# Decays without GpSimd, and key norms formed with the tokens on the partitions, in an RWKV and grid-attention block

## What is computed

```python
dx = token_shift(h) - h
x_r, x_w, x_k, x_v, x_a, x_g = (h + dx * mu[i] for i in range(6))
r = x_r @ w_in[:, c[0]:c[1]]          # k, v, g likewise from x_k, x_v, x_g
w_lo = jnp.tanh(x_w @ w_in[:, c[4]:c[5]])
a_lo = x_a @ w_in[:, c[5]:c[6]]
w_raw = (w0 + w_lo @ w_up).astype(f32)
log_decay = -jnp.exp(-jax.nn.softplus(-w_raw) - 0.5)
a = jax.nn.sigmoid((a0 + a_lo @ a_up).astype(f32))
kk = heads(k * k_k)                    # 16 heads of 64
kk = kk / jnp.maximum(jnp.sqrt(jnp.sum(kk * kk, axis=-1, keepdims=True)), 1e-12)
k = k * (1.0 + (a - 1.0) * k_a)
# recurrence over the tokens with r, decay, k, v, kk, kk * a; group norm;
# plus a bonus: sum(r * k * r_k) * v; times silu(g); @ w_out
```

## Time and profile before

| | us |
|---|---|
| median of 3 runs | 852.97 |
| lowest and highest run | 852.89, 855.48 |
| profiled execution, whole time | 856.66 |
| its span (first to last instruction) | 854.9 |
| TensorE busy in the span | 767.1 (90%) |
| VectorE, ScalarE, GpSimd busy | 501.7, 301.5, 213.0 |

### The profile page before, as it was taken

The page is one execution under the profiler, slowest core; times in us unless marked ns, Lnnn a source line. Parts: engine busy times, 40 slices in busy tenths (PEclk is TensorE's granted clock), DMA queues, the critical chain, the costliest instruction groups (busy, mean ns, idle before and its releaser), DMA issues.

```text
span 854.9 us, 17443 instructions
## 1 busy us (share of the span) xinstructions
PE 767.1 (90%) x7500; PEld 619.0 (72%) x7500; DVE 501.7 (59%) x800; ACT 301.5 (35%) x627; POOL 213.0 (25%) x163
## 2 busy tenths in 40 slices
PE   2599999799699698888876899999997999998997
PEld 2188777677578587778864788887775777776697
DVE  3983898888958622345745212631896676663611
ACT  6334542455522112233342134611333444433300
POOL 0164430444724212223211000370000000001652
PEclk9799999899889778989987999999998999999999
DMA  8023234223246764430004041601221111122131
GB/s 234 25 75 99 74 92 129 74 75 82 69 98 134 184 209 143 136 110 10 4 3 148 4 144 67 125 25 50 75 84 40 50 50 50 51 98 75 62 100 50
DMA packets 116621, 72.82 MB, mean 85 GB/s; under 512 B 26816, under 2 KB 113984, under 8 KB 116544
## 3 DMA queue, kind: packets, MB, share of 16 engines
q1 hardware_dynamic: 98496, 65.12, 26.4%
q10 hardware_dynamic: 18048, 6.58, 3.2%
HBM read 64.35 MB, written 7.34 MB: 84 GB/s over the span
## 4 chain that ended last, share of the span: by engine, by line
PE 76%; DVE 14%; issue 3%; ACT 3%; DMA 2%; POOL 1%; ACTq 0%; POOLq 0%; DVEq 0%
PE bank L515 19%; PE bank L954 8%; PE bank L509 6%; PE bank L511 6%; PE bank L510 6%; DVE arena L1498 3%; PE bank L622 2%; DVE arena L1550 2%; PE bank L978 2%; PE bank L991 2%; PE bank L671 2%; PE bank L755 2%; PE bank L654 2%; PE bank L1073 1%; PE bank L1075 1%
## 5 line engine op out<-in xcount | busy, mean ns | idle before, releaser
L515 PE MATMUL bank<-arena 128*128 128x256 f32 (+1 forms) x768 | 183.5, 398 | 4.5 <-DVE arena L1648 3.1
L515 PEld LDWEIGHTS bank<-arena 128*128 128x128 f32 x768 | 147.6, 195 | 38.1 <-issue 15.4
L1912 POOL TENSOR_TENSOR w_lo<-arena,w_hi 128x1024 fp32r<-128x1024 f32 x24 | 62.5, 2604 | 110.1 <-ACT w_hi L1156 110.1
L509 PE MATMUL bank<-x_hi,w_hi 128*128 128x512 f32 x192 | 80.2, 418 | 4.9 <-DVE x_lo L1504 4.9
L1156 ACT ACTIVATE w_hi<-arena 128x1024 fp32r<-128x1024 f32 x44 | 46.5, 1058 | 87.7 <-DMA arena<-w_in 86.3
L511 PE MATMUL bank<-x_hi,w_lo 128*128 128x512 f32 x192 | 76.8, 400 | 0.0
L510 PE MATMUL bank<-x_lo,w_hi 128*128 128x512 f32 x192 | 76.5, 399 | 0.0
L2017 POOL COPY arena<-arena 128x512 f32<-128x512 f32 x4 | 2.5, 614 | 195.4 <-DVE arena L1822 195.4
L509 PEld LDWEIGHTS bank<-x_hi,w_hi 128*128 128x128 f32 x192 | 37.0, 193 | 15.7 <-issue 7.7
L510 PEld LDWEIGHTS bank<-x_lo,w_hi 128*128 128x128 f32 x192 | 37.1, 193 | 9.9 <-issue 1.7
L1739 DVE TENSOR_TENSOR w_lo<-arena,w_hi 128x1024 fp32r<-128x1024 f32 x20 | 25.0, 1250 | 32.1 <-ACT w_hi L1156 32.1
(11 more groups left out here) (245 smaller groups left out, 1674.4 us busy)
## 6 DMA issues: line engine op xcount, KB each, us to landing
arena<-w_in SPq DMA_DIRECT2D x45, 512.0 KB, 3.9
arena<-w_ada SPq DMA_DIRECT2D x12, 1024.0 KB, 5.6
arena<-w_in SPq DMA_DIRECT2D x8, 1024.0 KB, 5.5
arena<-w_out SPq DMA_DIRECT2D x8, 1024.0 KB, 5.2
lt_dram<-arena ACTq DMA_DIRECT2D x16, 256.0 KB, 2.3
arena<-x SPq DMA_DIRECT2D x4, 512.0 KB, 7.4
arena<-x SPq DMA_DIRECT2D x1, 2048.0 KB, 7.9
out<-arena SPq DMA_DIRECT2D x8, 256.0 KB, 2.1
```

What stands on the lines that cost most here:

```text
L509: mm(o[:, :], w_hi[:, wk], x_hi, start=(k == 0), stop=False)
L515: last = mm(o, lhs(k), rhs(k), start=(k == 0), stop=(k == n - 1))
L1912: TT(WLO[n % 3][:, :], WR[n % 3][:, 0:1024], WHI[n % 3][:, :].bitcast(f32), SUB)\
```

## The change

Four things change together.

1. **Start.** The constants come in two DMAs, the small first one with what the start needs. Two of the four squares move to VectorE (L1536), one root and one reciprocal serve all four pieces, two of the four scalings move to ScalarE (L1185). The mixes for `w` and `a` are no longer formed: GpSimd multiplies their weights by `mu` once (`WMU`, L1987), and TensorE adds `h @ W` and `dx @ WMU` (32 matmuls for 16). `dx`, the mix for `k`, its rounding and its remainder are interleaved tile by tile.
2. **Key norms.** Four matmuls (L568) with the squares as the stationary side and two columns of the block matrix give sums of 128 tokens x 8; ScalarE's root, VectorE's maximum and reciprocal work on 128 x 8; ScalarE spreads the result (`spread_norm`), TensorE turns it back with four transposes (`turn_norm`, L552), and VectorE multiplies out of PSUM (`norm_k`).
3. **Decays.** L1920, L1923, L1927 and L1930 leave GpSimd: ScalarE forms `1 + (a - 1) * k_a` from the tanh, VectorE does the three products; the step `0.5 + 0.5 * tanh` for `a` is folded into other instructions, and `r * k` has two buffers.
4. **Second block.** The second half of the `v` projection stands behind `k` and `q`, with the last head norm inside it; the weight stream follows.

The heart of it, cut:

```diff
-            for c in range(KT):
-                for m in range(2):
-                    mix(m, c)
-            for c in range(KT):
-                mix(2, c)
-            for c in range(KT):
-                split_mix(2, c)
+            for c in range(KT + 2):
+                if c < KT:
+                    stored(dve, ("hT", c))
+                    TT(DX[:, c, :], HT[:, c, 0:T], HT[:, c, 1:T + 1], SUB).then_inc(dx_ready, 1)
+                if 1 <= c <= KT:
+                    dve.wait_ge(dx_ready, c)
+                    mix(2, c - 1)
+                if c >= 2:
+                    split_mix(2, c - 2)
...
             for k in range(KT):
-                pe.wait_ge(mixed, 2 * (k + 1))
-                for m in range(2):
-                    last = mm(o[side[m], :], w[:, k, 64 * m:64 * m + 64], MIXES[m][:, k, :], start=(k == 0),
-                              stop=(k == KT - 1), skip_group_check=True)
+                pe.wait_ge(dx_ready, k + 1)
+                for wk, x in ((w, HT[:, k, 1:T + 1]), (WMU, DX[:, k, :])):
+                    for m in range(2):
+                        last = mm(o[side[m], :], wk[:, k, 64 * m:64 * m + 64], x, start=(k == 0 and wk is w),
+                                  stop=(k == KT - 1 and wk is WMU), skip_group_check=True)
...
-                        ins = mm(o[:, :], heads1, SQ2[c % 2], start=True, stop=True)
-                        ins.then_inc(bank_full[where["kss", c][0]], 1)
+                        for t in range(NT):
+                            last = mm(o[:, 2 * t:2 * t + 2], SQ2[c % 2][:, t * P:(t + 1) * P], heads1[:, 0:P:HD], start=True,
+                                      stop=True, skip_group_check=True)
+                        last.then_inc(bank_full[where["kss", c][0]], 1)
+                        if c:
+                            turn_norm(c - 1)
...
+            def turn_norm(c):
+                pe.wait_ge(k_spread, c + 1)
+                o = out_bank(("kn", c), 6)
+                for t in range(NT):
+                    last = nc.tensor.transpose(o[:, t * P:(t + 1) * P], KNORM[c][:, t * P:(t + 1) * P], ident)
+                full(last, ("kn", c))
...
+            def spread_norm(c):
+                act.wait_ge(k_inverse, c + 1)
+                if c >= 2:
+                    arrived(act, ("kn", c - 2))
+                A(KNORM[c].rearrange("p (t n) -> p t n", n=HD), KINV[c % 2].unsqueeze(2).broadcast_to([P, 2 * NT, HD]), ACT.Copy)\
+                    .then_inc(k_spread, 1)
...
-                own.own(TS(ROOT[c % 2], ROOT[c % 2], 1e-12, None, MAX))
-                own.own(nc.vector.reciprocal(ROOT[c % 2], ROOT[c % 2]))
-                TT(AR[:, 0, c, :], AR[:, 0, c, :], ROOT[c % 2], MUL).then_inc(kk_done, 1)
+                own.own(TS(KINV[c % 2], KINV[c % 2], 1e-12, None, MAX))
+                nc.vector.reciprocal(KINV[c % 2], KINV[c % 2]).then_inc(k_inverse, 1)
                 mix(5, c)
+                if c:
+                    norm_k(c - 1)
...
+                A(KMOD, AB[:, c, :], ACT.Identity, bias=NKA[:, c:c + 1], scale=HKA[:, c:c + 1]).then_inc(kmod_ready, 1)
...
-                own.own(TT(AB[:, c, :], AB[:, c, :], AR[:, 0, c, :], MUL))
+                own.did(STT(AB[:, c, :], AB[:, c, :], 1.0, AR[:, 0, c, :], ADD, MUL))
+                own.own(TT(KB[:, c, :], KB[:, c, :], KMOD, MUL))
...
+                TT(RKT[c % 2], KB[:, c, :], AR[:, 1, c, :], MUL).then_inc(rk_ready, 1)
...
+                TT(KB[:, c, :], KB[:, c, :], E2, MUL).then_inc(kappa_ready, 1)
...
-            for nb in range(2):
+            def project_v(nb):
...
+                    if nb and b3 == 0:
+                        head_norm(len(items) - 1)
+
+            project_v(0)
             for name in ("kk", "q"):
                 for c in range(4):
                     qk_output(name, c, None, None)
-            head_norm(len(items) - 1)
+            project_v(1)
```

197 lines of the change are left out of this document (112 added, 85 removed).

## The result

The changed kernel took 820.0 us (median of 4 runs, 815.3 to 825.0), the kernel before 854.2 in the same comparison (4 runs, 852.9 to 859.3): a ratio of 0.959, 95% interval 0.952 to 0.966. The forecast was 821.1, range 813.5 to 829.0. A second comparison, with 4 and 7 runs, gave 0.9596 (0.953 to 0.966). The profiled execution took 819.92 us, its span is 818.0 us; that of before was 854.9.

The account below looks back on a forecast made before the run. TensorE was taken as the bound (76% of the chain), with time won at its waits and low clock; -8.7 - 1.5 + 4.1 - 16.4 - 1.8 - 7.6 = -31.9 from the median 852.97 gave 821.1 us, range 813.5 to 829.

Parts of the forecast that it names:

- Start: Before the split products of `k`: fewer mixes, interleaved, and earlier transposes start `k` at 32.9 for 41.6, -8.7 us.
- The pass at 0.43 us: Low-rank projection: 32 matmuls run as 32 passes at 0.43 us each, 13.8 us in all.
- The rival of a half low-clock projection: Start keeps half of its cost, by low clock in the projection or collisions and late arrivals: 827; chance 0.14.
- The collision: GpSimd's two `WMU` products meet VectorE's scalings of x: 1.1 us each, 2.2 if both are hit, not in the sum.
- The 823.2 that the exclusive lock gave: Whole-kernel time if the skill's VectorE-GpSimd port lock makes both collisions at the start certain.
- Clock of `k`: Eight tiles of `k`: with no wait ahead of them, less time at the low clock, -1.5 us.
- Key norms: TensorE in the `r` tiles: four added transposes per tile, sums unchanged at 0.86; +4.1 us, bounds -4.8 and +1.4.
- The rival of cheap sums: Key-norm sums cost only the rows' lower bound or the skill's issue floor: 816; chance 0.06.
- Decays: From the end of `r` to `g`: TensorE's waits of 11.6 and some 4.8 of low clock go, -16.4 us.
- 0.4 us to spare: Eighth decay tile: the triangular product needs 10.9 and comes at 11.3, so nothing waits.
- `g`: Stage ended by VectorE, which waits for the second gate: that comes at 11.8 instead of 13.6, -1.8 us.
- Second block: Before the second scores: TensorE's 5.7 us wait goes, plus 1.9 of low clock after it, -7.6 us.

Follow-up runs that it names:

- the second time: The changed kernel run once more, not altered: 822.1 us (median of 4, 815.9 to 827.1).

## Why the prediction was right

**Start**: predicted 13.7, 19.1 and 32.9 for transposes, projection and `k`; measured 13.26, 19.64 and 33.53, and 32.70 the second time. The x pieces land in 5.6 us instead of 7.4 (the page's DMA issues), which was not in the sum, and the 1.6 taken off ahead of the transposes had no row to rest on; it was 2.0. The transposes took 6.45 instead of 5.4, since the clock rose only 5.6 us after they began. The pass at 0.43 us was right to 1%: the projection took 13.89. The rival of a half low-clock projection did not come. The collision did, but once and not twice, since VectorE's first scaling began 0.06 us ahead of GpSimd's product and only the second one was delayed: 0.8 us for 2.2, and ScalarE's scaling hid them. GpSimd lost too: its two products took 3.04 us together, and 1.05 each where they stood alone.

```profile
10.97 3.04 POOL L1987 TENSOR_TENSOR arena<-arena 128x512 f32<-128x512 f32 x2 [10.53 <-DMA arena<-w_in]
```

The 823.2 that the exclusive lock gave in the prediction (821.1 and 2.2 make 823.3) was too high for that reason; each engine waiting in turn is what such a lock would do.

**Clock of `k`**: 2.1 for 1.5; the undone start confirms 2.0.

**Key norms**: +3.4 for +4.1, off by 0.7. The rows of the sums and the turns in the changed kernel:

```profile
89.27 0.95 PE L568 MATMUL bank<-arena 128*128 128x2 f32 x8
90.08 0.64 PE L552 MATMUL bank<-arena 128*128 128x128 f32 x4
90.47 0.48 PE L518 MATMUL bank<-x_hi,w_hi 128*128 128x512 f32 x1
```

From start to start the eight passes of the sums take 0.81, the four transposes 0.39. The 0.86 taken for the sums, "no change", was right to 0.05, and the 0.52 for a turn, taken from 8 records in 1.03 in another place, was a third too high. The rival of cheap sums is out: eight passes with 2 moving columns cost 0.10 us each, as much as each of the transposes with 128 beside them. The floor of about 25 ns that the Trainium skill gives (TensorE: Matmul & The Clock Gate, "Back-to-back issue gap") is not what sets these sums; the same section says that in a stream of weight loads and matmuls both set the spacing, and 0.10 agrees with that.

**Decays**: 83.7 for 82.7; without the last turn, -15.3 for -16.4, the largest miss outside the recurrence. The tail's "0.4 us to spare" was the step that failed, with a wait of 0.6, and the reason was not in it: a remainder of GpSimd's on VectorE's first step, 1.8 us. Without it, 82.87, and 82.44 where the last turn was gone too. The two causes that the prediction named together, VectorE's late start and GpSimd's products, can be told apart: the one decides at the stage's beginning, the other at its end.

**`g`**: -2.4 and -0.9 in the two traces, for -1.8; the wait before the recurrence was 3.9, not 4.9. The second gate, on which the term rests, came 12.8 us after `g` began and the second time 13.9, not 11.8. So its step failed, most or all of the gain arose behind that gate, and where was not taken apart: the size was right by luck.

**Second block**: -8.0 for -7.6 behind the scores, and undoing it gave 8.2.

**Base**: the sum stood against one profiled execution, 856.66, and was carried over to a median of 852.97. That base was low: beside the changed kernel the kernel before had medians of 854.2 and 856.1, and in the other comparisons 856 to 860. From the first two the sum gives 822.3 and 824.2, where 820.0 and 822.1 were measured: it was 2 us short both times, which the chance of the recurrence can account for but no run shows. The term list was right; the hit to 1 us was partly luck.

**The sum's blind spot** was the recurrence, taken at no change, with no width of its own: 14.5 us between the shortest and the longest trace, nearly the 15.5 of the whole range.

## What to carry to other kernels

When a wait goes, look for each wait's own cause: the two waits put down to GpSimd's product had different causes, the first of them a queue of work on VectorE that nobody needed yet; moving that work a few instructions ahead did as much as the new norms, at no cost in TensorE's time. Compare an instruction's time with its neighbours of the same form: 2.42 us for 18 columns, beside 0.22 for 32, says at once that something holds it up, here GpSimd's instruction, and the engine's busy time hides it. Judge an edit by the length of its own stage in the trace, since a stage that swings by 14 us hides 3 us in any median of a few runs.

## What the runs showed of the hardware

A VectorE product that met an instruction of GpSimd's ended only with it or just after (2.42 us for one that takes 0.18), and so did a step with a single operand in SBUF (2.19 for 0.43), but not a gate with one operand in a bank (0.69 for 0.69). With 128 stationary columns, a float32 pass of TensorE with 2 moving columns cost 0.10 us, as a transpose of 128 did. The recurrence, many matmuls of mostly 32 to 128 columns with waits of 0.5 to 3.4 us between them, ran 30 to 58 us of its 163 to 178 at 1.2 GHz, and not the same in two executions of one program (38.0 and 34.8); stages in which TensorE never stood still, such as `r` here, ran at 2.4 GHz throughout.
